# Two transformer blocks with expert layers on one core: slot table built by TensorE, router logits over column quarters, seven of eight row blocks of the first experts split, residual rows kept in DRAM

## The reference, cut to what matters

```
logits = h @ w_router + b_router            # 512 x 32; second block 512 x (4 + 16)
top_val, top_idx = top_k(logits, 4)         # second block: 2 of 16
gates = softmax(top_val)
# sort the 2048 (token, expert) pairs by expert, pad each expert to blocks of 128 slots
dest = pad_start[sorted_e] + (ar - start[sorted_e])
buf_tok[dest] = flat_tok[order]             # slot -> token
for each block of 128 slots, expert e:
    u = h_pad[tok] @ w1[e] + b1[e]          # 128 x 1024 by 1024 x 2048
    glu, lin = min(u[:, 0::2], 7), clip(u[:, 1::2], -7, 7)
    act = glu * sigmoid(1.702 * glu) * (lin + 1)
    y = act @ w2[e] + b2[e]                 # 128 x 1024 by 1024 x 1024
out[tok] += y * gate
x = x + mod * out
```

## Time and profile before

| | us |
|---|---|
| median of 3 runs (lowest, highest) | 3337.42 (3335.2, 3340.08) |
| the profiled execution | 3329.02 |
| its span, first to last instruction | 3327.3 |
| TensorE busy | 2672.4 (80%) |
| VectorE busy | 1677.5 (50%) |
| ScalarE busy | 1280.5 (38%) |
| GpSimd busy | 387.6 (12%) |
| mean granted clock of TensorE | 0.884 |

### The profile page before, as it was taken

One profiled execution on the slowest core, in us unless ns is written; L12 is line 12 of the kernel. 1 busy time (PEld: TensorE's weight loads), 2 busy tenths in 40 slices (PEclk: granted clock), 3 DMA queues, 4 the chain that ended last, 5 costly groups with the idle time before them and its releaser, 6 DMA issues. The chain is left out here.

```text
span 3327.3 us, 34291 instructions
## 1 busy us (share of the span) xinstructions
PE 2672.4 (80%) x11374; PEld 1781.7 (54%) x11374; DVE 1677.5 (50%) x2241; ACT 1280.5 (38%) x2236; POOL 387.6 (12%) x290
## 2 busy tenths in 40 slices
PE   6677639838999999999999996699399267664992
PEld 2276427625666666666666664589366137553441
DVE  0033545426667666666676666422666664541114
ACT  1032345314554444454544443222466404321331
POOL 0000000022112111121121112000000021001111
PEclk7788769959999999999999998799699588785996
DMA  9820800119999999999999995420000000313994
GB/s 349 296 97 24 286 19 1 57 36 389 360 341 351 346 352 351 353 350 345 341 352 346 352 352 202 143 84 28 4 1 1 1 1 7 108 39 126 335 371 172
DMA packets 367588, 671.12 MB, mean 202 GB/s; under 512 B 31560, under 2 KB 99528, under 8 KB 367469
## 3 DMA queue, kind: packets, MB, share of 16 engines
q1 hardware_dynamic: 354064, 630.08, 52.6%
q0 software_dynamic: 13440, 39.93, 3.4%
HBM read 611.71 MB, written 58.26 MB: 201 GB/s over the span
## 5 line engine op out<-in xcount | busy, mean ns | idle before, releaser
L1777 PE MATMUL psum<-weight_slots,turned 128*128 128x512 f32 x792 | 357.5, 594 | 3.7 <-ACT x_high L1833 3.7
L1874 DVE TENSOR_TENSOR w_low<-more,w_high 128x2048 fp32r<-128x2048 f32 x99 | 265.1, 2678 | 119.7 <-ACT w_high L1846 119.7
L663 PE MATMUL psum<-high 128*128 128x512 f32 (+3 forms) x832 | 292.8, 352 | 36.9 <-DVE low L685 36.9
L663 PE MATMUL psum<-low,high 128*128 128x512 f32 (+3 forms) x832 | 291.8, 351 | 0.0
L663 PE MATMUL psum<-high,low 128*128 128x512 f32 (+3 forms) x832 | 291.7, 351 | 0.0
L1874 DVE TENSOR_TENSOR w_low<-weight_slots,w_high 128x2048 fp32r<-128x2048 f32 x99 | 254.5, 2598 | 36.1 <-ACT w_high L1846 36.1
L1783 PE MATMUL psum<-w_high,x_high 128*128 128x512 f32 x528 | 259.8, 492 | 0.0
L1852 ACT ACTIVATE sig<-glu 128x256 f32<-128x256 f32 x132 | 55.0, 417 | 524.9 <-DVE glu L1885 524.9
L1777 PE MATMUL psum<-more,act_turned 128*128 128x512 f32 x528 | 237.5, 592 | 0.0
L685 DVE TENSOR_TENSOR low<-weight_slots,high 128x1024 fp32r<-128x1024 f32 (+3 forms) x84 | 89.2, 1066 | 291.7 <-ACT high L679 291.4
L1846 ACT CAST w_high<-weight_slots 128x2048 fp32r<-128x2048 f32 x99 | 187.7, 1897 | 113.5 <-PE psum L1787 113.4
(11 more groups left out here) (440 smaller groups left out, 4821.3 us busy)
## 6 DMA issues: line engine op xcount, KB each, us to landing
weight_slots<-in_w_mlp SPq DMA_DIRECT2D x99, 2048.0 KB, 12.7
more<-in_w_mlp SPq DMA_DIRECT2D x99, 2048.0 KB, 10.6
slot_rows<-y SPq DMA_DIRECT2D x51, 512.0 KB, 11.9
weight_slots<-in_w_ada SPq DMA_DIRECT2D x12, 2048.0 KB, 13.6
weight_slots<-in_w_mod SPq DMA_DIRECT2D x12, 2048.0 KB, 14.2
slot_rows<-zeros SPq DMA_DIRECT2D x1, 24576.0 KB, 74.6
weight_slots<-in_w_in SPq DMA_DIRECT2D x9, 2048.0 KB, 8.3
weight_slots<-in_w_gate SPq DMA_DIRECT2D x36, 512.0 KB, 6.8
```

Of the source, the lines that this page charges most:

```text
L663: mm = pe.matmul(psum[:, p.group % 8, 0:p.width], *p.operands(x, weights[:, n % 2], u * QK_ + kc, kc), start=p.first and u == 0 and kc == ...
L1777: pe.matmul(psum[:, bank, :], x[:, kc, :], slots[c][:, kc, :], start=kc == 0, stop=False)
L1874: dve.tensor_tensor(b.w_low[:, c % 2], slots[c][:, SK:, :], b.w_high[:, c % 2].bitcast(F32), ALU.subtract).then_inc(s.low_made, 1)
```

## The change

It has six parts.

1. `places` builds the table in SBUF. For each choice j VectorE makes two one-hot matrices, `is_at` (place within the block, 128 wide) and `is_block` (which block, times the token's number), and TensorE sums their products over tokens; the result, `slot_token`, is 128 places by blocks. Zeros, scatter DMAs and the DRAM table are gone. The counts are made ahead of the positions, and some waits between VectorE's steps are left out. VectorE also makes `shares`, gate by token and expert.
2. `logits_of` holds w (32 columns, padded in the second layer) and streams the 512 tokens, one column quarter of the array for every fourth row block; ScalarE copies, and four matmuls with `join` add the quarters.
3. `gather_tokens`: GpSimd copies one column of the table in SBUF, then gathers. No DMA for the numbers.
4. `first_expert_blocks`: one row block of each chunk stays float32 (WHOLE), seven are split. A chunk has two units, of 3 and 4 split row blocks; a block has twelve units, in the order (0,0) (0,1) ... (3,0) (3,1) (4,0) (5,0) (4,1) (5,1), here numbered 0 to 11. `w_high` and `w_low` have three places of one unit (AHEAD). High of unit n waits until TensorE has done unit n - 3. SyncE reloads a chunk when its low part is made. ScalarE, not VectorE, keeps y, without the bias.
5. b2 is added in `combine` by TensorE: `shares` times b2, into PSUM, which VectorE adds in the first step of each token tile.
6. The buffers of the block (rows, turned, act, y) lie in `k.x`. x itself is stored to DRAM ahead of the norm and loaded again in `combine`.

The core of the diff:

```diff
@@ places
+            for t in range(TX):
+                mm = pe.matmul(ps_count[0:experts, 0:1], mask[:, t, :], k.ones[:, 0:1], start=t == 0, stop=t == TX - 1)
+            mm.then_inc(s.counted, 1)
...
+            for j in range(top):
+                pe.wait_ge(s.found, j + 1)
+                for t in range(TX):
+                    mm = pe.matmul(ps_table[:, 0:n_blocks + 1], b.is_at[:, j, t, :], b.is_block[:, j, t, :],
+                                   start=j == 0 and t == 0, stop=j == top - 1 and t == TX - 1)
+            mm.then_inc(s.tabled, 1)
...
+            for j in range(top):
+                step.later(dve.tensor_tensor(b.is_at[:, j], spread(k.numbers[:], 1, TX),
+                                             b.at[:, j, :].unsqueeze(2).to_broadcast([P, TX, P]), ALU.is_equal))
+                step(dve.tensor_tensor(b.is_block[:, j], spread(k.numbers[:, 0:n_blocks + 1], 1, TX),
+                                       b.blockf[:, j, :].unsqueeze(2).to_broadcast([P, TX, n_blocks + 1]), ALU.is_equal))
+                step.reach(dve.tensor_tensor(b.is_block[:, j], b.is_block[:, j],
+                                             b.ids[:].unsqueeze(2).to_broadcast([P, TX, n_blocks + 1]), ALU.mult),
+                           s.found, j + 1)
...
-            for t in range(TX):
-                for j in range(top):
-                    i = t * top + j
-                    pool.indirect_dma_start(r.slot_token, bass.IndirectOffsetOnAxis(ap=r.dest[:, i:i + 1], axis=0),
-                                            b.ids[:, t:t + 1], None).then_inc(s.scattered, 16)
-            pool.wait_ge(s.scattered, 16 * (1 + TX * top))
@@ logits_of
+            for kc in range(DC):
+                g = kc % groups
+                mm = pe.matmul(psum[g * 32:(g + 1) * 32, 0, :], b.w[:, kc, :], turned[:, kc, :], start=kc < groups,
+                               stop=kc >= DC - groups)
+            mm.then_inc(s.summed, 1)
+            pe.wait_ge(s.kept, 1)
             for t in range(TX):
-                for kc in range(DC):
-                    mm = pe.matmul(psum[:, 0, t * width:(t + 1) * width], turned[:, kc, t * P:(t + 1) * P],
-                                   b.w[:, kc, :], start=kc == 0, stop=kc == DC - 1)
+                mm = pe.matmul(psum[:, 1, t * 32:(t + 1) * 32], c.partial[:, t * P:(t + 1) * P], k.join[:], start=True,
+                               stop=True)
@@ gather_tokens
-    pool.dma_start(b.slot_ids[:], r.slot_token[ds(block_no * P, P), :] if not isinstance(block_no, int) else
-                   r.slot_token[block_no * P:(block_no + 1) * P, :]).then_inc(s.gathered, 16)
-    pool.wait_ge(s.gathered, value + 16)
+    pool.tensor_copy(ids, r.slot_token[:, ds(block_no, 1)] if not isinstance(block_no, int) else
+                     r.slot_token[:, block_no:block_no + 1]).then_inc(s.ids_made, 1)
+    pool.wait_ge(s.ids_made, block_no + 1)
@@ first_expert_blocks, SyncE
+                        sync.wait_ge(s.unit_done, (i - 1) * U + (number[(c, 0)] + 1 + AHEAD))
+                        sync.sem_inc(s.taken, 1)
+                        sync.wait_ge(s.low_made, (i - 1) * U + (number[(c, 1)] + 2))
@@ TensorE
+                for n_ in range(U):
+                    unit(n_)
+                    if n_ in (3, 5, 7):
+                        turn_activations((n_ - 3) // 2)
+                    if n_ == 7:
+
+                        pe.wait_ge(s.gathered, i * 16 + 32)
+                        turn_rows(i)
@@ ScalarE
+            def rest(i):
+                for u in range(AHEAD, U):
+                    make_high(i, u)
+                    if u in (4, 6, 8):
+                        squash(i, (u - 4) // 2)
+                    if u in (6, 8, 9, 10):
+                        keep_activations(i, (6, 8, 9, 10).index(u))
+                    if u == 9:
+                        squash(i, 3)
+                    if u == 11:
+                        keep_rows(i + 2, 0, DC)
@@ VectorE
+            def rest(i):
+                for u in range(AHEAD, U):
+                    make_low(i, u)
+                    if u in (3, 5, 7, 9):
+                        clip(i, (u - 3) // 2)
+                    if u in (4, 6, 8):
+                        activate(i, (u - 4) // 2)
+                    if u in (7, 8, 9, 10):
+                        keep_activations_low(i, u - 7)
+                    if u == 9:
+                        activate(i, 3)
@@ combine
+            if x_rows is not None:
+                for t in range(TX):
+                    sync.dma_start(k.x[:, t], x_rows[t * P:(t + 1) * P, :]).then_inc(x_loaded[t], 16)
+            if bias is not None:
+                sync.dma_start(b.bias[:], bias).then_inc(s.bias_loaded, 16)
             sync.dma_start(b.gate[:], on_all(rows[0:1, 5 * D:6 * D])).then_inc(s.gate_loaded, 16)
```

More of the change, by code:

```diff
@@ L1502, in _ @@
             for t in range(TX):
[L1503 to L1504 removed]
+                (step if t == TX - 1 else step.later)(dve.scalar_tensor_tensor(
+                    out=b.pos[:, t], in0=ps_start[:, 0:experts], scalar=float(P), in1=b.pos[:, t], op0=ALU.mult,
+                    op1=ALU.add))
             for j in range(top):
[L1506 removed]
@@ new lines, in _ @@
+            step(dve.tensor_copy(r.dest[:], b.dest[:].rearrange("p j t -> p t j")))
+            for j in range(top):
+                share = r.gates[:, :, j:j + 1].to_broadcast([P, TX, experts])
+                step(dve.tensor_tensor(r.shares[:] if j == 0 else b.prod[:, 0], oneh[:, j], share, ALU.mult))
+                if j:
+                    step(dve.tensor_tensor(r.shares[:], r.shares[:], b.prod[:, 0], ALU.add))
+            dve.wait_ge(s.listed, 1)
+            step.later(dve.tensor_scalar(r.blocks[0:1, 0:n_blocks], ps_blocks[0:1, 0:n_blocks], float(experts - 1), None,
+                                         ALU.min))
@@ new lines, in _ @@
+            keep_rows(1, 0, DC)
+            keep_x_high(1)
+            for u in range(AHEAD):
+                make_high(0, u)
+            with act.Fori(0, last) as i:
+                rest(i)
+                for u in range(AHEAD):
+                    make_high(i + 1, u)
+                    if u == 0:
+                        keep_x_high(i + 2)
+                    else:
+                        keep_y(i, u - 1)
+            rest(last)
+            keep_x_high(last + 2)
+            for c in range(YC):
+                keep_y(last, c)
@@ L1907, in second_expert_blocks @@
+            make_x_low(2)
+            for u in range(AHEAD):
+                make_low(0, u)
+            with dve.Fori(0, last) as i:
+                step.restart()
+                rest(i)
+                for u in range(AHEAD):
+                    make_low(i + 1, u)
+                    if u == 0:
+                        make_x_low(i * 5 + 7)
+            step.restart()
+            rest(last)
+            make_x_low(last * 5 + 7)
 def second_expert_blocks(core, k, r, rows, y_rows, args, n_blocks):
@@ L2168, in _ @@
                 share = r.gates[:, t, j:j + 1]
-                if j == 0:
+                if j == 0 and bias is not None:
+                    dve.wait_ge(s.biased, t + 1)
+                    ins = dve.scalar_tensor_tensor(out=b.total[:], in0=b.got[:, i % ahead], scalar=share,
+                                                   in1=bias_ps[:, t], op0=ALU.mult, op1=ALU.add)
+                elif j == 0:
                     ins = dve.tensor_scalar(b.total[:], b.got[:, i % ahead], share, None, ALU.mult)
```

435 lines of the change are left out of this document (240 added, 195 removed).

## The result

The changed kernel takes 3351.49 us (median of 4 runs, 3349.93 to 3361.6) against 3336.31 for the kernel before (the three runs of the table ahead and a fourth): ratio 1.0055, 95% interval 1.0037 to 1.0074. So it is slower by half a per cent, where I had forecast 3301 and a gain. The profiled execution has a span of 3359.9 us, the longest of the four runs.

A forecast was written before the change was run, and what follows sets the result against it. It took TensorE to bound the first experts' loop before, and a ring of waits after. Routing -44, loop +1, copies at the start +1 and combine +6 gave -36 us: 3301 us on the medians' scale, range 3281 to 3323.

The forecast's parts named there:

- the ring: First experts' loop: chain of waits through VectorE, TensorE and ScalarE sets the block's period, 39.15 us; chance 0.55.
- TensorE's sum: First experts' loop: TensorE's own work per block falls to 35.8 us, 3.3 below 39.1.
- VectorE's phase of 23.30: Loop: `w_low` of units 3 to 9, clips, act and low activations 0 to 2, without a pause, 23.30 us.
- My bounds for the ring: Loop: the block's chain of waits could be 0.6 us shorter or 0.7 longer, -20 to +25 us.
- wait and hold at unit 10: Loop, `w_low` of unit 10: 1.10 us idle, then 3.48 instead of 2.29 against the broadcast, together 4.58 us.
- gaps of up to 1.7 us: Loop, TensorE: 3.3 us more waiting per block, before unit 10 and turned activations, with clock 1.00.
- rival (2): Loop: TensorE's clock falls in its gaps, ending slower; 3383 us at 30% of its part; chance 0.12.
- My sign for this rival: A TensorE clock under 0.97 in the first experts' loop would prove that the clock falls in gaps.
- The two table loads: Loop, ScalarE: two loads of 1.28 us per block fall into its idle time, as before.
- The hold by the broadcast: Loop: the broadcast makes `w_low` of unit 10 take 3.48 us, ending 4.30 after the broadcast's start.
- Routing: Both layers: logits gain 5.5 and 7.5 us, places 15.3 and 10.9, gathers 2 and 3; sum 44.2.
- Combine: First layer: VectorE starts 5 us later, waiting for the gate row behind x and b2; +6 us (2 to 9).

The follow-up runs named there:

- e4: Changed kernel with ScalarE's loop begun one unit later, so the table load falls before high of unit 4, not unit 3; 3349.99 us.
- e6: Changed kernel with two row blocks of each chunk whole and units of 2 and 4 split ones; 3273.4 us.
- e2: Changed kernel with the bias broadcast put behind `w_low` of unit 2 and the bias row's load behind chunk 1; 3318.25 us.
- e5: Edit of e2 on the changed kernel, and ScalarE keeps half of the turned rows earlier, before the sigmoid of chunk 3; 3281.77 us.
- e1: Changed kernel with 14 throwaway matmuls of 384 columns in TensorE's gap before unit 10; 3315.65 us.
- the second profile: Changed kernel run and profiled once more with no edit; 3348.21 us, span 3347.0 us.
- e3: Changed kernel with the loop of the kernel before (four row blocks whole), x kept in SBUF and b2 added in the loop; 3280.9 us.
- e9: Changed kernel with the first combine's loads in the order gate, b2, x; 3347.77 us.
- e7: Edit of e6 on the changed kernel, with the bias broadcast put behind `w_low` of unit 2; 3275.41 us.
- e8: Edits of e6, e2 and e5 together on the changed kernel, with the gate row loaded first in the first combine; 3242.53 us.

## Why the prediction was wrong

**That the ring sets the period, not TensorE's sum: right.** e4 shortens the ring and the short blocks by 0.36, and e6 moves the period down against TensorE's sum. That ScalarE has a second ring just behind VectorE's I had not seen: it is why e2 gave 39.85 and not 38.3, and e5, which shortens both, 38.64. In the block from 1268.18 to 1308.18 of the changed kernel the steps that I had laid out take, measured beside forecast: from `w_low` of unit 3 to unit 10 on TensorE 24.57 + 4.45 = 29.02 (28.35); units 10 and 11 5.57 (5.40); whole row block, unit 0 and the start of high of unit 3 3.47 (3.47); high 1.94 (1.93). Sum 40.00 against 39.15.

**The term that was too small: VectorE's phase of 23.30.** It is 24.57 less the wait of 0.61, so 23.96. I had read a clip as ending at the next act, and the other operations as joining without a pause; the rows have 0.09 more for each of four clips and 0.1 for each of three acts (the fourth ends in the wait), which is the 0.66 but for a few hundredths. With 0.17 more for units 10 and 11 it makes the ring 0.83 longer, 27 us over 33 blocks, of which VectorE's phase is 22. My bounds for the ring named it ("a wait costs 0.1 more at each of eight handovers"), as the upper end; the ring went just past that. The sum of wait and hold at unit 10, 4.58, was exact, 0.61 + 3.97, but its parts were not (1.10 + 3.48 forecast): they cancel because the end of the held `w_low` is set by the broadcast, not by when it starts.

**The step that failed: "the clock 1.00" in "gaps of up to 1.7 us".** The gap before unit 10 was 2.4, and most of the difference was in my own numbers. By the prices of the prediction VectorE has, from the end of act(2) to unit 10, 0.33 + 1.67 + 1.84 + 0.33 + 0.45 + 4.58 + 0.33 + 0.14 = 9.67 us (low activations 1, `w_low` of unit 9, clip(3), low activations 2, act(3), wait and hold, low activations 3, start), and TensorE has 0.34 + 0.90 + 2 x 2.89 + 0.34 = 7.36 us (two pairs of turned activations, the turned rows, units 8 and 9). That leaves 2.3, not the 1.5 that I wrote; my 5.8 was the two units alone, without what is turned between them. The rows have 9.86 (1302.76 to 1312.62) for the first sum, so only 0.2 came from VectorE's being late; by the same count the gap in the rows is 2.5 to 2.6, and 2.4 from the end of the last record. In two blocks of three the clock fell at this gap, for 19 x 1.55 = 29 us. This was rival (2), to which I gave 0.12. Alone it costs 0.95 to 1.06 us a block, just under the 1.1 at which I had it take away the whole gain, and e1, which has the longer ring but not the fall, is faster than before; the two together made the kernel slower. My sign for this rival, a clock under 0.97 in the loop, would have missed it: the mean is 0.97 and 0.98, and only the single blocks show it. My error was to weigh the clock by the busy share of the loop, 92%, which says nothing of how the 8% are spread. The Trainium skill, page "TensorE: Matmul & The Clock Gate", section "What's actually happening", has the lower clock as the default that activity releases. The rows at 1312 to 1318 agree, with the clock at 0.50 behind the gap and at 1.00 again under the work that followed; I had quoted the page for the rival and not followed it to the one wait where it would act.

**The two table loads "fall into ScalarE's idle time": wrong by 0.35 us.** `w_high` of unit 3 starts at 1281.67, right behind the load, and e4 has the short block 0.36 shorter without it. It did not add to the sum because I had allowed 0.42 for the end of unit 0.

**The hold by the broadcast: right, and the Trainium skill's rule nearly.** `w_low` of unit 10 began 0.33 us into the broadcast and ended 2.00 us after its end, 4.30 after its start, as in the earlier trace rows. By the Trainium skill's rule ("SBUF — State Buffer", "Who interferes with whom") it would run its whole 2.29 after the broadcast's end, an estimate 0.29 too long. e2 shows 2.00 at unit 3.

**Routing: right, a little better.** Forecast 20.8 and 18.4 to the first loads, measured 22.7 and 19.3 (22.2 and 19.3 in the second profile); the logits of the first layer took 3.7 us in place of the 6.0 that I took, as their 16 records took 1.92 and not 3.64. The 3.64 of the earlier trace rows was taken at a granted clock of 0.50, and the 1.92 ran at 1.00; in the second layer the same 16 records ran at 0.50 and took 3.64. That was luck: I had not looked at the clock behind the price. The second loop gained 5.5: its first store of y comes 4.0 sooner after the first load, where I had 3 for the gathers, and 1.5 come from one later block, 12.93 us long before and 11.39 now, whose cause is open. The first loop gained 4.0 in e3, where I had 2. The table matmuls took 7.06 and 3.61, forecast 6.9 and 3.4. e3 shows the sum: 53 us by the medians, just above my bounds of 30 to 52.

**Combine: +10 for a forecast of +6 (2 to 9).** VectorE began 15.3 us after the first load, 9.1 later than before, where I had 5. I had it wait for the gate row; in the rows the wait that ends last is TensorE's product with b2, which began 11.4 us after the first load and held VectorE for 3.9 more, at a granted clock of 0.50. My sum had no term for it. 4.4 of the 10 are the order of the loads (e9).

**Sum.** Forecast -44 + 1 + 1 + 6 = -36. Measured, by the second profile: -22.2 - 19.3 - 5.0 + 56.3 + 9.5 and +0.4 elsewhere, together +19.7; by the medians +15.2.

## What to carry to other kernels

When work is taken from the engine that binds and given to the others, lay the ring of waits out end to end, with the pause between two operations read from a row for each kind of handover, and find the single place where the binding engine's new idle time gathers: on TensorE a gap of 2.4 us cost 1.4 to 1.6 us more in two blocks of three and oftener, while gaps of 1.33, 0.96 and 0.7 us cost nothing. Where two rings are within a few tenths of each other (VectorE's and ScalarE's here), shortening one shows nothing (e7) until the other is shortened too (e8). The best split of a shared task lies where the engines' sums and the rings meet: two of eight row blocks whole (e8, ratio 0.9717) beat both one (e5, 0.9831) and four (e3, 0.9849). Three were not tried.

## What the runs showed of the hardware that I had not expected

- TensorE's clock fell at the gap's end or behind it, not early in it: in the changed kernel's first profile it fell at 20 gaps of 2.4 us, 9 times in the last 0.5 us of the gap and 11 times up to 0.5 us after work had begun again, and stayed at 0.50 for 3.3 to 3.5 us each time. (In the second profile one fall came 1.3 us behind the gap.) It went in a regular pattern: after one or two long blocks came a short one (three long ones once in the second profile, three or seven in e4), although the gap was 2.36 to 2.47 us in all of them. So the gap's length alone does not say whether the clock falls.
- A `w_low` (two inputs in SBUF) that meets a broadcast of GpSimd ends 2.0 us after the broadcast does, whenever it began: started 0.33 us into it (the changed kernel), 0.82 (before), 1.31 (e2) or 1.68 (e5), it ended 2.00 or 2.01 us after it.
- GpSimd's copy of one column, 128x1, took 2.20 us in the loop, and ended with the `w_low` beside it (1272.19 and 1272.15); at the start of the stage, alone, it took 0.19:

```profile
729.93 0.19 POOL L1711 COPY slot_ids<-slot_token 128x1 int32<-128x1 int32 x1 [19.84 <-remote]
```
